# Gate maps of a two-block transformer kernel: odd maps' gated one-hots made by VectorE in one step, ScalarE scaling only the even maps'

## What is computed

```
e = i1 * N_KEYS + i2                         # T x 8 heads x 16
gate = softmax(best, axis=-1)
act = gelu(einsum("thkd,td->thk", u_exp[e], xb))
out = einsum("thk,thkd->td", gate * act, v_exp[e])
```

## Time and profile before

| | |
|---|---|
| median of 3 runs | 2598.82 us (2598.51 to 2599.08) |
| the profiled execution | 2607.07 us, its span 2605.0 us |
| PE / PEld busy | 2330.1 us (89%) / 2239.9 us (86%) |
| VectorE (DVE) busy | 1741.7 us (67%) |
| ScalarE (ACT) busy | 1291.1 us (50%) |
| GpSimd (POOL) busy | 253.5 us (10%) |
| L401, GpSimd's one-hots | 256 operations, 212.3 us |
| L936, ScalarE's scalings | 512 operations, 162.7 us |

### The profile page before, as it was taken

One profiled execution on the slowest core, in us unless ns is written; L12 is line 12 of the kernel. 1 busy time (PEld: TensorE's weight loads), 2 busy tenths in 40 slices (PEclk: granted clock), 3 DMA queues, 4 the chain that ended last, 5 costly groups with the idle time before them and its releaser, 6 DMA issues.

```text
span 2605.0 us, 53888 instructions
## 1 busy us (share of the span) xinstructions
PE 2330.1 (89%) x18096; PEld 2239.9 (86%) x18096; DVE 1741.7 (67%) x3632; ACT 1291.1 (50%) x2842; POOL 253.5 (10%) x286
## 2 busy tenths in 40 slices
PE   3887789999997699999889988799999976999998
PEld 3785579999996599999879946799999975999998
DVE  6665554888877955565633456638888869655555
ACT  3345244545556745455534554345555457545554
POOL 3000000000006900000010000000000049100000
PEclk7998789999998999999989979899999999999999
DMA  8761134555551055555434402345555520455554
GB/s 313 258 234 54 45 130 148 178 180 187 181 185 49 0 186 181 182 185 179 137 106 161 169 1 81 123 144 184 180 178 184 185 81 0 139 184 182 180 185 145
DMA packets 106072, 389.62 MB, mean 150 GB/s; under 512 B 12032, under 2 KB 12160, under 8 KB 105232
## 3 DMA queue, kind: packets, MB, share of 16 engines
q1 hardware_dynamic: 104688, 381.73, 42.8%
q10 hardware_dynamic: 992, 4.88, 0.5%
q0 software_dynamic: 320, 2.13, 0.2%
HBM read 387.64 MB, written 1.05 MB: 149 GB/s over the span
## 4 chain that ended last, share of the span: by engine, by line
PE 81%; POOL 8%; DVE 6%; ACT 3%; DMA 1%; issue 1%; SPq 0%; ACTq 0%; POOLq 0%; DVEq 0%
PE ps L533 19%; PE ps L502 16%; PE ps L497 16%; PE ps L499 15%; PE ps L537 9%; POOL scores L401 8%; DVE big L1113 1%; DMA big<-ada_in 1%; PE ps L612 1%; PE ps L592 1%; DVE act_lo L1166 1%; DVE lo L1090 1%; PE ps L602 1%; PE ps L640 1%; PE ps L491 1%
## 5 line engine op out<-in xcount | busy, mean ns | idle before, releaser
L827 ACT ACTIVATE hi<-raw 128x512 fp32r<-128x512 f32 x1356 | 776.2, 620 | 88.9 <-PE ps L502 87.1
L1090 DVE TENSOR_TENSOR lo<-raw,hi 128x512 fp32r<-128x512 f32 x844 | 551.7, 695 | 193.7 <-ACT hi L827 192.7
L497 PE MATMUL ps<-act_hi,hi 128*128 128x256 f32 x3376 | 557.6, 288 | 83.6 <-DVE act_lo L1166 41.8
L502 PE MATMUL ps<-act_hi,lo 128*128 128x256 f32 x3376 | 554.7, 287 | 26.1 <-DVE lo L1090 26.1
L497 PEld LDWEIGHTS ps<-act_hi,hi 128*128 128x128 f32 x3376 | 478.3, 197 | 90.2 <-DVE act_lo L1166 68.4
L499 PE MATMUL ps<-act_lo,hi 128*128 128x256 f32 x3376 | 553.4, 287 | 0.0
L533 PE MATMUL ps<-act_hi,hi 128*128 128x256 f32 x2048 | 513.9, 283 | 0.0
L533 PE MATMUL ps<-act_lo,hi 128*128 128x256 f32 x2048 | 513.5, 283 | 0.0
L502 PEld LDWEIGHTS ps<-act_hi,lo 128*128 128x128 f32 x3376 | 476.4, 196 | 28.9 <-DVE lo L1090 28.8
L499 PEld LDWEIGHTS ps<-act_lo,hi 128*128 128x128 f32 x3376 | 476.9, 196 | 0.0
L852 ACT ACTIVATE big<-ps 128x256 f32 (+1 forms) x354 | 135.8, 383 | 592.1 <-PE ps L502 592.1
(11 more groups left out here) (176 smaller groups left out, 1361.5 us busy)
## 6 DMA issues: line engine op xcount, KB each, us to landing
raw<-u SPq DMA_DIRECT2D x256, 512.0 KB, 3.3
raw<-v SPq DMA_DIRECT2D x256, 512.0 KB, 3.4
raw<-front SPq DMA_DIRECT2D x166, 512.0 KB, 3.2
big<-ada_in SPq DMA_DIRECT2D x48, 512.0 KB, 5.5
big<-biasA_in ACTq DMA_DIRECT2D x1, 2048.0 KB, 10.2
xT<-xT_in ACTq DMA_DIRECT2D x1, 1024.0 KB, 9.4
big<-keys_in ACTq DMA_DIRECT2D x1, 1024.0 KB, 13.6
scores<-memT_in POOLq DMA_DIRECT2D x1, 1024.0 KB, 6.7
```

The source lines that it names most:

```text
L497: pe.matmul(out_ap, hi_l(k), hi_r(k), start=(first and k == 0), stop=False, skip_group_check=True)
L502: mm = pe.matmul(out_ap, lo_l(k), hi_r(k), start=False, stop=(last and k == n - 1), skip_group_check=True)
L827: act.activation(hi[:, s, :, :], raw[:, rs, 4 * h:4 * h + 4, :], ACT.Copy).then_inc(hi_done, 1)
L1090: dve.tensor_tensor(lo[:, s, :, :], raw[:, rs, 4 * h:4 * h + 4, :], hi[:, s, :, :].bitcast(F32), ALU.subtract).then_inc(lo_done, 1)
```

## The change

In the odd maps VectorE no longer makes the four tokens' `gatehot` with one compare for ScalarE to scale. It makes it token by token, with one `tensor_scalar` each that compares `iota` with the token's i2 column and multiplies by its gate column, and counts a new semaphore `hot_fused`. ScalarE scales the even maps only, and `hot2` and `hot_gate` count even maps only. TensorE waits for `hot_fused` in odd maps and `hot_gate` in even ones. GpSimd's program and the matmuls are the same.

```diff
@@ gate_map (TensorE)
-                        pe.wait_ge(hot_gate, n + 1)
+                        pe.wait_ge(hot_fused if j % 2 else hot_gate, g * (MAPS // 2) + (32 * (b - 1) + j // 2 + 1))
@@ gate_hots (ScalarE)
-                    for j in range(MAPS):
-                        act.wait_ge(hot2, g * MAPS + (64 * (b - 1) + j + 1))
+                    for j in range(0, MAPS, 2):
+                        act.wait_ge(hot2, g * (MAPS // 2) + (32 * (b - 1) + j // 2 + 1))
@@ hots (VectorE)
-                    key = chosenT[:, 1, bass.ds(g * 4 * MAPS + 4 * j, 4)]
-                    dve.tensor_tensor(gatehot[:, j, :, :], iota[:, :].unsqueeze(1).broadcast_to([P, 4, P]),
-                                      key.unsqueeze(2).broadcast_to([P, 4, P]), ALU.is_equal).then_inc(hot2, 1)
+                        key = chosenT[:, 1, bass.ds(g * 4 * MAPS + 4 * j, 4)]
+                        dve.tensor_tensor(gatehot[:, j, :, :], iota[:, :].unsqueeze(1).broadcast_to([P, 4, P]),
+                                          key.unsqueeze(2).broadcast_to([P, 4, P]), ALU.is_equal).then_inc(hot2, 1)
+                    else:
+                        for t in range(4):
+                            tok = g * 4 * MAPS + (4 * j + t)
+                            ins = dve.tensor_scalar(gatehot[:, j, t, :], iota[:, :], chosenT[:, 1, bass.ds(tok, 1)],
+                                                    chosenT[:, 2, bass.ds(tok, 1)], ALU.is_equal, ALU.mult)
+                        ins.then_inc(hot_fused, 1)
```

More of the change, by code:

```diff
@@ L299, in two_blocks_kernel @@
         hot2, hot_gate = sem("one_hots_i2"), sem("one_hots_gated")
+        hot_fused = sem("one_hots_gated_at_once")
         wmap, w_done = sem("gate_map"), sem("gate_map_applied")
```

## The result

The changed kernel takes 2614.40 us (median of 4, 2611.12 to 2616.27) against 2598.95 us of the kernel before beside it (median of 4): ratio 1.0055, interval 1.0038 to 1.0072. It is slower, by about 15 us or 0.55%; forecast were 26, in a range of 2600 to 2665 us that holds the measured time.

What follows compares the result with a forecast made beforehand. GpSimd was taken to bound the kernel at 3.29 us per pair, then VectorE at 2.40 + 1.03 + 0.37 = 3.80. The stages' +12.8 and +13.3 gave +26.1: 2624.9 us, range 2600 to 2665.

Steps and rivals of the forecast that it cites:

- GpSimd sets the pace before, by contention with VectorE's two-input one-hots: Gate-map stages before: VectorE operations with two SBUF inputs hold GpSimd's reads back, 0.97 of 3.29 us per pair.
- ScalarE's relief gains nothing: Removing 4 of 8 ScalarE scalings per pair gains nothing, since they hide under VectorE and GpSimd.
- Four small operations cost 1.03 in place of 0.60: VectorE, odd maps: four 128x128 tensor_scalars at 0.257 us each replace one 128x512 one-hot of 0.60.
- The addresses: One address computation ahead of each small VectorE operation, costed at nothing; if limiting, the four at 0.32 us each.
- VectorE becomes the bound, GpSimd idles: Changed stages: VectorE sets 3.80 us per pair; GpSimd needs 3.4 and idles before its first operation of a map.
- Collisions of 2.5 x 0.15 = 0.37: Two or three GpSimd operations per pair fall among VectorE's small ones, each costing VectorE 0.15 us.
- The end of a stage without waits, 2.49 us: The last four applies of each stage take 2.49 us, never waiting for TensorE.
- TensorE's clock: A thinner TensorE may be granted less than the stretch's 0.94 clock; costed at nothing, VectorE having four maps in hand.
- Alternation: Rival: each small VectorE operation waits for a whole GpSimd operation, 5.83 us per pair, 2746.7 us; 6%.
- One column per cycle: Rival: small VectorE operations take 0.324 us each without collisions, 3.70 per pair, 2618.9 us; 5%.
- The case without collisions: Rival: small VectorE operations slip between GpSimd's, 3.43 us per pair, 2602.8 us; 11%.
- The faster case: Rival: small VectorE operations cost 0.13 us each, GpSimd is held back less, 3.10 per pair, 2582.9 us; 6%.

Runs made afterwards that it cites:

- e1: Kernel before, with GpSimd computing odd-map one-hots for the first group only and just signalling afterwards (output wrong): 3.01 us per pair, ratio 0.9920.
- e4: Kernel before, with VectorE's 128x512 one-hots reading iota from a PSUM copy, all work done: 2.99 us per pair, ratio 0.9932.
- e3: Changed kernel with odd maps' i2 one-hots again one VectorE compare, left ungated; ScalarE scales even maps only: 3.24 us per pair, ratio 0.9994.
- e2: Changed kernel with GpSimd silent after the first group, odd maps reusing that group's one-hots: 3.43 us per pair, ratio 1.0016.
- e9: Changed kernel measured again, without edits: 3.55 us per pair, ratio to the kernel before 1.0031.
- e6: Changed kernel with even maps' one-hots and the four tensor_scalars all reading iota from PSUM: 3.67 us per pair, ratio 1.0073.
- e5: Changed kernel with only the even maps' two one-hots reading iota from PSUM, tensor_scalars still from SBUF: 3.47 us per pair, ratio 1.0031.
- e8: On top of e4, GpSimd makes odd maps' gated one-hots by compare and multiply, VectorE their i1 one-hots: 3.02 us per pair, ratio 0.9952.

## Why the prediction was right

The direction, the engine that bounds the changed kernel and the price of its small operations were right. The size was twice too large: +26.1 us forecast, +13.0 in the stages. The range held it because it was wide, from +1 to +66 us.

- *GpSimd sets the pace before, by contention with VectorE's two-input one-hots.* Shown: taking its work away gives 3.01 per pair (e1), taking the contention alone away gives 2.99 with all the work done (e4). The profile's own attribution, 31.5 us of TensorE's waits put down to VectorE's apply in the first stage, pointed elsewhere; the reading by starts and ends was the right one.
- *ScalarE's relief gains nothing.* Shown by e3, but for at most 2.5 us.
- *Four small operations cost 1.03 in place of 0.60.* 0.256 each measured (e2) against 0.257. The addresses were put at nothing, and nothing of them shows.
- *VectorE becomes the bound, GpSimd idles.* As forecast: GpSimd's first operation of a map waits 0.5 to 1.3 us. Its work was put at 3.4 per pair; it is 2.8.
- *Collisions of 2.5 x 0.15 = 0.37.* This is the term that was mis-sized: 0.14 (3.57 - 3.43). All of the 0.37 was put among the small operations. Two or three of GpSimd's operations do fall there, as forecast, but together they cost 0.08 (0.04 in e9), 0.02 to 0.03 each and not 0.15. The row behind the 0.15 is of a VectorE operation with two SBUF inputs, and was no measure for a small one. The other 0.06 (0.09 in e9) is at the even one-hots, where the prediction had nothing, because GpSimd's burst comes later than was thought: it starts about 2.2 us behind the even apply in place of 1.3, and its last operation reaches into the next period's even one-hots. The prediction had GpSimd start half of the 2.05 us of matmuls after the last small operation; but TensorE makes the even map first and waits for ScalarE to have scaled it, and GpSimd starts when both maps are done (851.22, above). That this wait is what makes the burst late is read from the timeline; no run tests it. With 0.14 the same sum gives 3.57 per pair and 26.1 - 60 x 0.23 = 12.3 us.
- *The end of a stage without waits, 2.49 us.* It is 2.87 (915.33 + 0.69 - 913.15): the last map comes 0.4 us later than the apply could take it, and the apply waits for TensorE (0.20 us in the view), which was forecast to happen nowhere. 0.8 us in all, on the other side.
- *TensorE's clock.* The granted clock was 0.98 in the stretch where it was 0.94: it was not granted less.
- *The rivals.* Alternation fell: the longest L1324 took 0.464, the mean 0.366, where a wait for a whole GpSimd operation would have added 0.60. One column per cycle fell (e2, e6). The case without collisions, 3.43, is what e2 measures, 0.14 below the changed kernel; in time it would have been +4 us. The faster case needed under 0.20 per small operation, and it is 0.256.

## What to carry to other kernels

Work should be taken off the engine that the stage waits for: here the change relieved the one engine with slack and paid on one that was full, and the price of the added operations could be read off a similar instruction's back-to-back spacing to 1%. What another engine's traffic adds to them could not: that term was put at 0.37 and is 0.14. Four short operations in place of one long one cost by their fixed part, 0.19 of each 0.256 us here, even where a column takes them half the time. Where GpSimd's identical instructions take 0.6 and 1.1 us by turns, look at what VectorE reads at that time; here moving a constant operand of it to PSUM was worth 0.7%, where this change lost 0.3 to 0.5%.

## What was not expected of the hardware

- A GpSimd operation among VectorE's short tensor_scalars costs them next to nothing (346 ns in e5 against 328 in e2) and itself little (612 ns in e5 against 601 in e4). The Trainium skill's rule for a GpSimd instruction and a VectorE one in a two-port mode (SBUF — State Buffer, section "Who interferes with whom"), exclusion for the whole instruction, did not show at this size. Where something like it does is for a VectorE tensor_tensor with two SBUF inputs beside a 128x4096 GpSimd operation: two of them took 8.14 us, where two took 1.29 just before (47.75).
- The second step of a tensor_scalar, with a second per-partition scalar, costs GpSimd 0.2 us on 128 columns (601 ns in e4, 804 in e8).
- A VectorE tensor_tensor costs the same with iota in PSUM as in SBUF (675 ns, e4; 672 ns undisturbed, e1).
